# Three attentions of a two-block model: the reciprocals of the softmax row sums move from VectorE to GpSimd, as a power of minus one

## The reference

```python
scores = jnp.where(valid[None, None, :, None, :], scores, -1e30)
probs = jax.nn.softmax(scores, axis=-1).astype(v.dtype)
out = jnp.einsum('bhcqk,bckhd->bcqhd', probs, vb)
...
s = s + cum[:, :, lo:hi, None] - cum[:, :, None, :hi]
s = jnp.where(kpos[None, :] <= qpos[:, None], s, -1e30)
prob = jax.nn.softmax(s, axis=-1).astype(v.dtype)
outs.append(jnp.einsum('bhqk,bhkd->bhqd', prob, v[:, :, :hi]))
```

## Time and profile before

| | us |
|---|---|
| median of 3 runs | 1594.95 |
| lowest and highest | 1594.84, 1595.11 |
| the profiled execution | 1595.21 |
| its span | 1593.3 |
| PE busy in the span | 1575.5 (99%) |
| PEld busy | 1322.3 (83%) |
| DVE busy | 1149.8 (72%) |
| ACT busy | 749.5 (47%) |
| POOL busy | 205.0 (13%) |

### The profile page before, as it was taken

How to read it: one execution, slowest core, us unless ns; L and a number is a source line. 1 busy time by engine, 2 the same in 40 slices (tenths; PEclk the granted TensorE clock), 3 DMA queues, 4 the chain that set the end, 5 groups by cost and what they waited for, 6 DMA issues and landing times.

```text
span 1593.3 us, 21775 instructions
## 1 busy us (share of the span) xinstructions
PE 1575.5 (99%) x8763; PEld 1322.3 (83%) x8763; DVE 1149.8 (72%) x1538; ACT 749.5 (47%) x1041; POOL 205.0 (13%) x281
## 2 busy tenths in 40 slices
PE   9999999999999999999999999999999999999998
PEld 7877777888888888888799987899888888888887
DVE  6755788668384865656768778578777866878857
ACT  6524575545252533424685256454444434444544
POOL 0001045200000000023610256000000000000000
PEclk9999999999999999999999999999999999999999
DMA  5484365775757546762144311344447347244321
GB/s 193 159 222 143 117 260 211 171 225 132 238 133 238 132 145 172 228 221 106 54 159 147 137 62 54 116 161 147 162 167 253 108 130 261 83 147 158 106 106 54
DMA packets 38164, 247.65 MB, mean 155 GB/s; under 512 B 5104, under 2 KB 7600, under 8 KB 12080
## 3 DMA queue, kind: packets, MB, share of 16 engines
q1 hardware_dynamic: 27728, 193.76, 32.7%
q0 software_dynamic: 5472, 39.85, 12.8%
q10 hardware_dynamic: 4864, 12.66, 2.2%
HBM read 235.73 MB, written 44.07 MB: 176 GB/s over the span
## 4 chain that ended last, share of the span: by engine, by line
PE 84%; DVE 8%; ACT 3%; issue 3%; POOL 1%; DMA 1%; DVEq 0%; ACTq 0%; POOLq 0%
PE bank L973 16%; PE bank L975 16%; PE bank L974 16%; PE bank L1395 3%; PE bank L1397 3%; PE bank L1396 3%; PE bank L1021 2%; PE bank L1023 2%; PE bank L1022 2%; PE bank L1500 2%; PE bank L1564 2%; PE bank L1565 2%; PE bank L1563 2%; PE bank L1501 2%; PE bank L1502 2%
## 5 line engine op out<-in xcount | busy, mean ns | idle before, releaser
L973 PE MATMUL bank<-a_hi,w_hi 128*128 128x512 f32 x968 | 381.1, 394 | 0.6 <-DVE x L2464 0.6
L975 PE MATMUL bank<-a_hi,w_lo 128*128 128x512 f32 x968 | 377.2, 390 | 0.0
L974 PE MATMUL bank<-a_lo,w_hi 128*128 128x512 f32 x968 | 376.9, 389 | 0.0
L2385 DVE TENSOR_TENSOR w_lo<-w_raw,w_hi 128x2048 fp32r<-128x2048 f32 x82 | 187.8, 2292 | 64.7 <-ACT w_hi L1690 64.5
L1690 ACT ACTIVATE w_hi<-w_raw 128x2048 fp32r<-128x2048 f32 x84 | 160.3, 1908 | 141.3 <-DMA w_raw<-in_strips 118.9
L975 PEld LDWEIGHTS bank<-a_hi,w_lo 128*128 128x128 f32 x968 | 181.7, 188 | 38.5
L973 PEld LDWEIGHTS bank<-a_hi,w_hi 128*128 128x128 f32 x968 | 181.8, 188 | 37.8 <-issue 2.0
L974 PEld LDWEIGHTS bank<-a_lo,w_hi 128*128 128x128 f32 x968 | 181.9, 188 | 35.8
L1395 PE MATMUL bank<-w_hi,t_hi 128*128 128x512 f32 x280 | 109.3, 390 | 0.1
L1396 PE MATMUL bank<-w_lo,t_hi 128*128 128x512 f32 x280 | 109.0, 389 | 0.0
L1397 PE MATMUL bank<-w_hi,t_lo 128*128 128x512 f32 x280 | 109.0, 389 | 0.0
(11 more groups left out here) (446 smaller groups left out, 3443.6 us busy)
## 6 DMA issues: line engine op xcount, KB each, us to landing
w_raw<-in_strips SPq DMA_DIRECT2D x91, 1024.0 KB, 4.8
a_part<-in_parts SPq DMA_DIRECT2D x25, 1024.0 KB, 7.6
a_part<-in_parts POOLq DMA_DIRECT2D x20, 1024.0 KB, 9.0
pre<-in_parts POOLq DMA_DIRECT2D x8, 1024.0 KB, 9.5
pre<-pre POOLq DMA_DIRECT2D x8, 1024.0 KB, 9.4
fold_raw<-pre SPq DMA_DIRECT2D x8, 1024.0 KB, 4.8
fold_raw<-in_parts SPq DMA_DIRECT2D x6, 1024.0 KB, 5.2
spare<-in_parts SPq DMA_DIRECT2D x5, 1024.0 KB, 15.5
```

Source lines behind the costliest of these rows:

```text
L973: mm(ps[:, :], w_hi[slot][:, k, cols], hi[:, k, :], start=(k == 0), stop=False)
L974: mm(ps[:, :], w_hi[slot][:, k, cols], lo[:, k, :], start=False, stop=False)
L975: return mm(ps[:, :], w_lo[slot][:, k, cols], hi[:, k, :], start=False, stop=(k == kt - 1))
L2385: v.tensor_tensor(w_lo[j], w_raw[j], w_hi[j].bitcast(F32), ALU.subtract).then_inc(strip_split, 1)
```

## The change

DVE's `invert` goes away in all three calls: 32 reciprocals of one column and 32 of two columns. POOL's `normalize` waits for `exped` of its tile in place of `inverted`, computes `row_inv = row_sum ** -1` itself with a two-input instruction on one column of 128 rows, waits for that instruction on its own semaphore, and then multiplies as before. The exponent stands in `wait_note[:, 1:2]`, which POOL sets to -1.0 in the prologue; the semaphore count that PE waits for before `small_columns` goes up by one accordingly. `lead_v` no longer calls `invert(0)`. Nothing else moves.

```diff
             pool.memset(w16, 0.0).then_inc(w16_ready, 1)
+            pool.memset(wait_note[:, 1:2], -1.0).then_inc(w16_ready, 1)
+            pool.wait_ge(w16_ready, 2)
...
                 def normalize(n):
                     w = P * (n % TT + 1)
-                    pool.wait_ge(inverted, INVERTED0[call] + (n // 2 + 1 if causal else n + 1))
+                    pool.wait_ge(exped, TILE0[call] + n + 1)
+                    pool.tensor_tensor(row_inv[:, n:n + 1], row_sum[:, n:n + 1], wait_note[:, 1:2], ALU.pow).then_inc(inverted, 1)
+                    pool.wait_ge(inverted, TILE0[call] + n + 1)
                     pool.tensor_scalar(score[n % len(score)][:, 0:w], score[n % len(score)][:, 0:w], row_inv[:, n:n + 1], 1.0,
                                        ALU.mult, ALU.mult).then_inc(normed, 1)
...
-                pe.wait_ge(w16_ready, 2 + which)
+                pe.wait_ge(w16_ready, 3 + which)
...
-                def invert(n, count=1):
-                    dve.wait_ge(exped, t0 + n + count)
-                    v.reciprocal(row_inv[:, n:n + count], row_sum[:, n:n + count]).then_inc(inverted, 1)
-
...
-                    if causal and 2 <= n <= TILES and n % 2 == 0:
-                        invert(n - 2, 2)
-                    if not causal and 2 <= n <= TILES:
-                        invert(n - 1)
...
-                    if m == 4:
-                        invert(0)
```

More of the change, by code:

```diff
@@ L507, in build @@
         HEAD0 = {"1": 0, "2a": HEADS8, "2b": 2 * HEADS8}
-        INVERTED0 = {"1": 0, "2a": TILES, "2b": TILES + TILES // 2}
         TILE0 = {"1": 0, "2a": TILES, "2b": 2 * TILES}
@@ L2554, in attention @@
                 if lead is not None:
-                    lead(stage, most, invert)
+                    lead(stage, most)
                 else:
@@ L2774, in add_ssd, with lead_v @@
                 v.tensor_tensor(x[:, j, :], x[:, j, :], bank[j % 2][:, :], ALU.add).then_inc(dve_evac, 1)
-            def lead_v(stage, most, invert):
+            def lead_v(stage, most):
                 dve.wait_ge(y_sq, 8)
```

## The result

| | median us | lowest and highest |
|---|---|---|
| before | 1595.03 | 1594.84, 1595.98 |
| changed | 1618.86 | 1614.36, 1619.77 |

The changed kernel takes 1.0145 of the time of the kernel before (95% interval 1.0133 to 1.0157), 23.8 us more. The forecast was 1594.0, "about the same"; the time lies in the range (1588 to 1636) and in the case that was called "POOL becomes the bound of the causal calls".

A forecast was written before the change was run, and what follows sets the result against it. PE was taken as the bound, busy 99% of the span; 5 us of stalls removed against 4 us of POOL overflow made net -1 us, so the median goes from 1594.95 to 1594.0, range 1588 to 1636.

The forecast's parts named there:

- POOL becomes the bound of the causal calls: Rival, 2a and 2b: powers overflow POOL; at X = 0.73, 16 us less 4 of gain, median 1607; chance 0.17.
- the overflow of the causal calls: In 2a and 2b POOL lacks room for 0.54 us more a tile: 7.8 us upper end, 4 us entered.
- the gain: PE's stalls on POOL at the transposes go: between 4.0 and 10.8 us, 5 us entered.
- nothing elsewhere: Outside the attentions no cost: the prologue's memset hides ahead of DMA sums, otherwise some 0.2 us.
- What bounds the kernel, and how a stall comes about: PE bounds, busy 99%; in call 1's tile 6, 1.89 us are DVE's queue, and PE idles 0.82 us.
- X: Time of one power on POOL, 96 of them in the three calls; taken as 0.45 us, far bound 1.2.
- The floor of 0.27: Lower bound for a power on POOL, in us, from one-input instructions of 128 and 512 columns.
- the forecast's own case: All three calls: X from about 0.35 to 0.55, 1591.8 to 1598.1 us; chance 0.30, no effect included.
- The room method: POOL's idle time less 0.09 us hand-overs, per tile: 0.80 us in call 1, 0.49 in 2a, 0.31 in 2b.
- The ports: Rival: powers wait for DVE's two-input instructions, 0.13 us each, X = 0.58 in effect; median 1601, chance 0.08.
- the next releaser: What is late next once tile 6 of call 1 comes sooner: PE's own queue, free at 235.85.
- the room of 0.80 us a tile: Call 1: POOL has 19.3 us for 24 tiles, so 0.54 us more a tile overflows nothing.

## Why the prediction was wrong

The prediction entered 4 us of overflow less 5 us of gain: -1. The span grew by 23.3 us: 16.8 in 2a and 2b, 1.4 in call 1 and 5.3 behind it, less 0.2. The step that failed is the overflow of the causal calls, of which only half was entered; two further terms failed beside it, the gain and the "nothing elsewhere".

**What bounds the kernel, and how a stall comes about:** right. PE's waits for POOL at the transposes were DVE's queue, and taking the reciprocal out of that queue removed them when POOL had room (PE has none left without a reciprocal).

**X:** taken as 0.45 us, measured 0.55 undisturbed. The floor of 0.27, extrapolated from one-input products, was too high (a two-input product of one column takes 0.19), and the arithmetic, guessed at 0.18, is 0.36. The two errors partly cancel. An X of 0.55 was still in the forecast's own case, with at most 1598.1, so this size is not what failed. Its mean of 0.627 is over the 0.6 from which the prediction called itself wrong.

**The overflow: the step that failed.** The prediction found 7.8 us of overflow at its X and took 4, on the ground that POOL's waiting for the port would shrink. It did not. Five heads of 2b now take 10.1 us of POOL each (the product of 128 columns starts at 955.49 in the second head and at 1006.20 in the seventh), where undisturbed durations make 5.45 + 4 x 0.55 + 13 x 0.09 = 8.8. 1.3 us a head are still lost to waiting, as against (26.55 - 21.8) / 4 = 1.2 before. The room method in full gives 0.15 x 28 + 0.33 x 28 = 13.4 us at 0.55. With the mean powers, 0.61 in 2a and 0.58 in 2b, it gives 0.21 x 28 + 0.36 x 28 = 16.0, and the measured loss is 16.8, net of the 1.7 us that the run without a reciprocal wins in these calls. So the method came near: the overflow had to be entered in full, with the power's own waiting in it.

**The ports:** this rival came about in part. By the rule of the Trainium skill (SBUF — State Buffer, Who interferes with whom) a power can be held up by DVE and hold DVE up. The trace agrees on the first: the powers last 0.08 us longer on average than undisturbed, where the rival took 0.13. DVE's instructions did not get longer, and the price of 1601 was not the outcome.

**The gain: mis-sized.** 5 us were entered for the stalls. The run without any reciprocal shows 1.6 for the whole of it. The prediction named the next releaser for tile 6 only, PE's own queue. For the other tiles it is DVE's `pt_lo`, 2.9 us in call 1, which the transposes wait for as well. PE's idle time by releaser was not what removing that releaser brought, and the weight loader's 10.8 us still less.

**"Nothing elsewhere": failed.** It weighed POOL's DMAs in the prologue, not the two behind call 1 (L812). An issue that moved by a microsecond relative to SP's cost 5 us. This stood in no rival.

**Call 1:** the room of 0.80 us a tile was taken as enough. It nearly was: 1.5 us of loss, where a net gain had been entered. With a mean of 0.68 a power and its hand-over take 0.77 us a tile, almost all of the room, and PE waits 4.1 us for POOL in call 1. Which tiles come late, and whether the copies at a head's start are why, was not tested.

**The chances:** slower had 0.42, the largest of the three, and the rival "POOL the bound" had the mechanism. It priced itself at 1607 for X = 0.73. The full overflow at 0.55 makes 1594.95 + 13.4 = 1608.4. With 3.4 more in the causal calls, 5.3 behind call 1 and 1.4 in it, that is 1618.5, against 1618.9 measured. That the time lies in the stated range is luck: the upper end was drawn for an X near 1.0.

## What to carry to other kernels

Before a small instruction goes to an engine that looks idle, count that engine's room in the stretch where it will run, hand-overs included, and enter the overflow in full. The waits that were in POOL's busy time before were there afterwards too (1.2 and 1.3 us a head), and the added instruction brought its own. The worth of a stall is what comes late next, and leaving the step out of the computation altogether measures its upper bound in one run: here 1.6 us. When an edit or an experiment shifts times by a microsecond, look for DMAs of different queues that were issued close together, and pin their order before judging the edit.

## What the runs showed of the hardware that was not expected

A power on GpSimd takes 0.55 us for one column of 128 rows and 0.70 for two, and a product of the same shape 0.19. The 16 powers of 0.6 us and more all began while VectorE was in an instruction with two inputs in SBUF. They took up to 1.40 us, and 13 of them ended 0.41 us behind that instruction.

A 1 MB strip load issued 0.3 to 0.9 us ahead of a summing DMA of GpSimd's queue landed in 4.7 to 4.8 us, and one issued 0.5 to 1.3 us behind it in 10.1 to 11.1 us, in four kernels each. Issued 0.47 us behind in the run with one power for two tiles (300.88 against 300.41), it took 8.1.

After a PE stall of 3.9 to 4.8 us the granted clock averaged 0.72 to 0.86 over the 12 us from 324 to 336 in four runs, and after one of 1.9 us (one power for two tiles) it stayed at 1.00.
